# Routing the experts of a mixture layer through 25 passes of one ranking instead of 26 passes of two

## What is computed

```
gate = p_group * softmax(top_v)                  # top-2 inside the chosen group
hb   = silu(xb @ w_gate[e]) * (xb @ w_up[e])     # 1024 -> 512, rows xb of expert e
out[token] += gate * (hb @ w_down[e])            # 512 -> 1024
```

## Time and profile before

| | us |
|---|---|
| median of 3 runs | 1451.56 (1447.0 to 1452.16) |
| the profiled execution | 1454.74 |
| its span, first to last instruction | 1452.9 |
| PE busy in the span | 1336.4 (92%) |
| DVE, ACT, POOL busy | 506.4, 251.5, 175.2 |
| mean granted TensorE clock | 0.956 |

### The profile page before, as it was taken

The page is one execution under the profiler, slowest core; times in us unless marked ns, Lnnn a source line. Parts: engine busy times, 40 slices in busy tenths (PEclk is TensorE's granted clock), DMA queues, the critical chain, the costliest instruction groups (busy, mean ns, idle before and its releaser), DMA issues.

```text
span 1452.9 us, 15254 instructions
## 1 busy us (share of the span) xinstructions
PE 1336.4 (92%) x5616; PEld 691.3 (48%) x5616; DVE 506.4 (35%) x1193; ACT 251.5 (17%) x487; POOL 175.2 (12%) x170
## 2 busy tenths in 40 slices
PE   6999999999999888879998679999999999999985
PEld 3444554644446566654555534443444444444432
DVE  2079683133546565651344512111111111111100
ACT  5000114132124333331111010000000000000000
POOL 1000005222000000000000011211212112112111
PEclk9999999899999899999999589999999999999998
DMA  6011010100120110302221098959999999999970
GB/s 256 0 60 58 1 58 0 58 6 6 48 66 5 36 35 5 121 1 93 101 87 73 28 395 338 400 195 350 424 404 406 412 407 391 402 397 389 403 272 18
DMA packets 51272, 261.70 MB, mean 180 GB/s; under 512 B 21571, under 2 KB 21843, under 8 KB 38908
## 3 DMA queue, kind: packets, MB, share of 16 engines
q1 hardware_dynamic: 42684, 243.72, 41.9%
q0 software_dynamic: 8320, 16.81, 4.7%
q10 hardware_dynamic: 192, 0.17, 0.1%
HBM read 247.52 MB, written 23.64 MB: 187 GB/s over the span
## 4 chain that ended last, share of the span: by engine, by line
PE 69%; issue 8%; DMA 7%; DVE 7%; POOL 3%; DVEq 3%; ACT 1%; SPq 0%; POOLq 0%; ACTq 0%
PE ps L1176 18%; PE ps L1178 13%; PE ps L895 9%; PE ps L1081 8%; PE ps L899 4%; DMA arena<-in_ex_up 3%; PE ps L1026 3%; DMA arena<-in_ex_down 2%; PE ps L1057 2%; POOL arena L2020 2%; PE ps L1042 2%; PE ps L1162 1%; PE ps L1102 1%; DMA arena<-in_ex_gate 1%; DVE arena L1495 1%
## 5 line engine op out<-in xcount | busy, mean ns | idle before, releaser
L1176 PE MATMUL ps<-arena 128*128 128x512 f32 x768 | 336.7, 595 | 1.9 <-ACT arena L1971 0.8
L1176 PEld LDWEIGHTS ps<-arena 128*128 128x128 f32 x768 | 144.3, 191 | 171.9 <-issue 169.3
L1178 PE MATMUL ps<-arena 128*64 128x512 f32 x480 | 213.5, 601 | 8.3 <-DMA arena<-in_ex_up 4.5
L1179 PE MATMUL ps<-arena 128*64 128x512 f32 x480 | 213.6, 601 | 0.0
L899 PE MATMUL ps<-arena 128*128 128x512 f32 x384 | 173.6, 605 | 0.0
L895 PE MATMUL ps<-arena 128*128 128x512 f32 x320 | 137.6, 592 | 0.0
L1740 DVE TENSOR_TENSOR arena<-arena,ps 128x512 f32<-128x512 f32 x26 | 17.9, 689 | 328.8 <-PE ps L1176 202.3
L1178 PEld LDWEIGHTS ps<-arena 128*64 128x64 f32 x480 | 64.7, 138 | 138.1 <-issue 136.2
L1081 PE MATMUL ps<-arena 128*128 128x512 f32 x256 | 112.1, 597 | 0.8 <-DVE arena L1532 0.8
L899 PEld LDWEIGHTS ps<-arena 128*128 128x128 f32 x384 | 72.6, 195 | 83.0 <-issue 81.5
L2076 POOL DMA_INDIRECT out<-arena x26 | 42.0, 1615 | 473.2 <-DVE arena L1746 473.2
(11 more groups left out here) (299 smaller groups left out, 1297.7 us busy)
## 6 DMA issues: line engine op xcount, KB each, us to landing
arena<-in_ex_gate SPq DMA_DIRECT2D x32, 2048.0 KB, 21.7
arena<-in_ex_up SPq DMA_DIRECT2D x32, 2048.0 KB, 24.2
arena<-in_ex_down SPq DMA_DIRECT2D x32, 2048.0 KB, 24.0
arena<-in_w_in SPq DMA_DIRECT2D x5, 2048.0 KB, 7.8
arena<-in_x SPq DMA_DIRECT2D x16, 512.0 KB, 6.2
arena<-bias_by_distance SPq DMA_DIRECT2D x4, 1024.0 KB, 5.9
arena<-in_w_out SPq DMA_DIRECT2D x8, 512.0 KB, 7.3
out<-arena SPq DMA_DIRECT2D x8, 512.0 KB, 2.6
```

The lines of the kernel that those rows point to most:

```text
L1176: last = mm(ps[:, to, :], rowsT[:, k, :], weights[left][:, k, cols], **f)
L1178: mm(ps[0:HALF, to, :], rowsT[:, k, 0:HALF], weights[left][:, k, cols], **f)
L1179: last = mm(ps[HALF:P, to, :], rowsT[:, k, HALF:P], weights[right][:, k, cols], **f)
```

## The change

`PASSES` is now built by `expert_passes()` from one ranking over all 32 experts, in units of 64 rows. There are 25 passes: 14 "whole" (W) for ranks 0 to 13, and 11 two-sided ones. Four of these (R) hold rows 129 to 192 of ranks 0 to 3 in the left half and ranks 14 to 17 in the right; seven (P) hold ranks 18 to 31 and, in one place, 17 with 18, two by two. The order is W R W R W R P W R W P W W P W P W W W W P W P W P; the last pass is two-sided (ranks 30 and 31).

With one ranking a token's two experts can stand in the two halves of one pass, and so its output row could be added to twice by one DMA. Therefore a two-sided pass is added in two steps: `add_pass(n, 0)` adds the left rows, and `add_pass(n, 1)` the right ones after the first has landed. DVE makes the two lists of rows (`side_rows`, in which the rows of the other side are out of bounds and so are skipped). There are 36 adds where there were 26. Between the two steps POOL fetches the gates of the next pass. The next gather stands behind the second step.

```diff
+    for kind in "WRWRWRPWRWPWWPWPWWWWPWPWP":
+        if kind == "W":
+            rank = next(whole)
+            passes.append(("whole", (rank, 0), None))
+            if rank < 4:
+                rests.append((rank, 1))
+        elif kind == "R":
+            passes.append(("halves", rests.pop(0), (next(one), 0)))
+        else:
+            passes.append(("halves", (next(one), 0), (next(one), 0)))
...
+        def sides_of(n):
+            return (0,) if PASSES[n][0] == "whole" else (0, 1)
+
+        def landed_from(u, last):
+            return 16 * sum(len(sides_of(n)) for n in range(last + 1) if n % 2 == u)
...
-                pe.wait_ge(codeT_done, 3)
-                for n in range(2):
-                    last = mm(ps[:, 5, 40 * n:40 * n + RANKED], codeT[0:2 * EXPERTS, n, :], perm[0:2 * EXPERTS, :],
-                              start=True, stop=True)
-                last.then_inc(order_mm, 1)
+                pe.wait_ge(codeT_done, 2)
+                both = slice(0, 2 * EXPERTS)
+                mm(ps[:, 5, 0:NP], codeT[both, :], perm[both, EXPERTS:EXPERTS + NP], start=True, stop=True)
+                right = EXPERTS + NP
+                mm(ps[HALF:P, 5, N_WHOLE:NP], codeT[both, 0:HALF], perm[both, right:RANKED], start=True, stop=True).then_inc(order_mm, 1)
...
-            ts(slots[:, 0:16], ps[:, 5, 0:16], -1.0, None, ALU.add)
-            for side in range(2):
-                rows = slice(side * HALF, (side + 1) * HALF)
-                pairs = ps[rows, 5, 40:40 + RANKED].rearrange("p (s two) -> p s two", two=2)[:, 8:18, side]
-                ts(slots[rows, 16:NP], pairs, -1.0, None, ALU.add)
+            ts(slots[:, 0:NP], ps[:, 5, 0:NP], -1.0, None, ALU.add)
             nc.vector.drain()
             rows_of_blocks(0, NP)
             nc.vector.drain().then_inc(slots_ready, 1)
+            ts(not_left, cst[:, C_TOK:C_TOK + 1], float(HALF), 4.0 * SEQ, ALU.is_ge, ALU.mult)
+            nc.vector.drain()
+            ts(side_f[:, 0], tok_f[:, N_WHOLE:NP], not_left, None, ALU.add)
+            ts(side_f[:, 1], tok_f[:, N_WHOLE:NP], not_left, 4.0 * SEQ, ALU.subtract, ALU.add)
+            nc.vector.drain()
+            nc.vector.tensor_copy(side_rows, side_f)
+            nc.vector.drain().then_inc(sides_ready, 1)
...
-            f(codeT[0:2 * EXPERTS, 0, :], ps[0:2 * EXPERTS, 5, 128:256], ACT.Copy).then_inc(codeT_done, 1)
-            f(codeT[0:2 * EXPERTS, 1, :].rearrange("p (r n) -> p r n", r=2),
-              ps[0:2 * EXPERTS, 5, 128:128 + HALF].unsqueeze(1).to_broadcast([2 * EXPERTS, 2, HALF]), ACT.Copy).then_inc(codeT_done, 1)
+            f(codeT[0:2 * EXPERTS, :], ps[0:2 * EXPERTS, 5, 128:256], ACT.Copy).then_inc(codeT_done, 1)
...
-            def add_pass(n):
-                add_rows(n, n % 2, 16 * ((n + 1) // 2), rows_of(n))
+            def add_pass(n, side):
+
+                u = n % 2
+                rows = rows_of(n)
+                if len(sides_of(n)) == 2:
+                    pool.wait_ge(sides_ready, 1)
+                    rows = side_rows[:, side, COLUMN[n] - N_WHOLE:COLUMN[n] - N_WHOLE + 1]
+                pool.wait_ge(y_v, n + 1)
+                if side:
+                    pool.wait_ge(y_out[u], landed_from(u, n) - 16)
+                else:
+                    at_least(pool, y_out[1 - u], landed_from(1 - u, n - 1))
+                nc.gpsimd.indirect_dma_start(out, bass.IndirectOffsetOnAxis(ap=rows, axis=0), ys[:, u, :], None,
+                                             bounds_check=SEQ - 1, oob_is_err=False, compute_op=ALU.add).then_inc(y_out[u], 16)
...
                 if n:
-                    add_pass(n - 1)
+                    add_pass(n - 1, 0)
                     pool.wait_ge(row_gate_in, 16 * n)
                 fetch_gates(row_gate[:, n:n + 1], dst_of[:, COLUMN[n]:COLUMN[n] + 1])
+                if n and len(sides_of(n - 1)) == 2:
+                    add_pass(n - 1, 1)
+
             def last_pass():
-                add_pass(NP - 1)
-                pool.wait_ge(y_out[(NP - 1) % 2], 16 * ((NP - 1) // 2 + 1))
+                for side in range(len(sides_of(NP - 1))):
+                    add_pass(NP - 1, side)
+                pool.wait_ge(y_out[(NP - 1) % 2], landed_from((NP - 1) % 2, NP - 1))
```

More of the change, by code:

```diff
@@ L60, with expert_passes @@
 NCONST = C_EJ + 256
[L62 to L67, removed]
+def expert_passes():
+    whole, one, rests = iter(range(14)), iter(range(14, EXPERTS)), []
+    passes = []
+    for kind in "WRWRWRPWRWPWWPWPWWWWPWPWP":
[8 more added lines that the diff above has]
+            passes.append(("halves", (next(one), 0), (next(one), 0)))
+    return passes
+PASSES = expert_passes()
 NP = len(PASSES)
@@ L70, with experts_of @@
 SLOTS = NP + EXTRA
[L71 to L80, removed]
-def weight_loads():
[L85 to L89, removed]
+HALF = P // 2
+BLOCKS = {"whole": ((0, P, 0),), "halves": ((0, HALF, 0), (HALF, P, 1))}
+OF_KIND = {kind: [n for n in range(NP) if PASSES[n][0] == kind] for kind in BLOCKS}
+BY_KIND = OF_KIND["whole"] + OF_KIND["halves"]
+COLUMN = [BY_KIND.index(n) for n in range(NP)]
+N_WHOLE = len(OF_KIND["whole"])
+RANKED = EXPERTS + 2 * NP - N_WHOLE
+def experts_of(n):
+    return [side[0] for side in PASSES[n][1:] if side]
+def weight_loads():
+    order = list(dict.fromkeys(s for n in range(NP) for s in experts_of(n)))
+    last = [max(n for n in range(NP) if s in experts_of(n)) for s in order]
     issues = []
@@ L140, in order_constants @@
     part, e = np.arange(P)[:, None], np.arange(EXPERTS)[None, :]
[L141 to L147, removed]
+    mine, block = part % EXPERTS, part // EXPERTS
+    sides = ([(s, 0) for s in range(EXPERTS)] + [PASSES[n][1] for n in BY_KIND] + [PASSES[n][2] for n in BY_KIND[N_WHOLE:]])
+    rank = np.array([s for s, _ in sides])[None, :]
+    of_block = np.array([b for _, b in sides])[None, :]
+    cols = [np.broadcast_to(EXPERTS - 1.0 - e, (P, EXPERTS)), (e == mine), np.where(block == of_block, rank, -1)]
     return np.ascontiguousarray(np.concatenate([np.asarray(c, np.float32) for c in cols], 1))
@@ L797, in _ @@
             sp.wait_ge(extras_ready, 1)
+            sp.wait_ge(down_mm, NP)
             def extra_weights(slot, u, pair):
@@ L1199, in down @@
                 at_least(pe, y_v, n)
-                left, right = landed_for("down", n)
+                blocks = landed_for("down", n)
                 for half in range(2):
-                    last = times_weights(5 + half, actT, FC, w_down, left, right, slice(half * 512, (half + 1) * 512))
+                    last = times_weights(5 + half, actT, FC, w_down, blocks, slice(half * 512, (half + 1) * 512))
                 last.then_inc(down_mm, 1)
@@ L1229, in extra @@
                 for half in range(2):
-                    last = times_weights(5 + half, actT, FC, w_down, u, u, slice(half * 512, (half + 1) * 512))
+                    last = times_weights(5 + half, actT, FC, w_down, [(0, P, u)], slice(half * 512, (half + 1) * 512))
                 last.then_inc(down_mm, 1)
```

101 lines of the change are left out of this document (55 added, 46 removed).

## The result

| | before | change |
|---|---|---|
| median, us | 1451.86 (4 runs, 1447.0 to 1455.32) | **1426.68** (4 runs, 1426.49 to 1429.05) |
| the profiled execution | 1454.74 | 1429.05 |
| its span | 1452.9 | 1427.2 |

Two later sets of runs of the same kernel gave 0.985 twice (1428.77 and 1428.13 us); by those two medians the time would lie just inside the range, at its lower end.

The account below looks back on a forecast made before the run. PE was taken as the bound by a small margin over the weight stream. Terms -22.2 + 2 - 0.6 + 0 + 6 = -14.8 us, from the median 1451.56 us, gave 1437 us, range 1428 to 1448 us.

Parts of the forecast that it names:

- the waits that were expected in the last pass: Last, two-sided pass: PE waits 0 to 5 us for up of rank 31 and 1 to 3 us for its down.
- the end (+6): After PE's last product: two one-sided adds instead of one, +3.5 us, plus pass 23's add; +6 us, bounds +3.5 and +11.
- the add of pass 23: Ahead of the last add: issued some 10 us before the last y_v, landing in 12.5 us, it costs 2.5 us.
- One pass fewer on PE, -22.2: Expert stretch on PE: 25 passes instead of 26, all else equal, save 22.2 us.
- Another order of the weights, +2: Weight stream: buffers come free at other times, waits total about 14 us instead of 11.8; +2 us, bounds -3 and +6.
- the four waits: PE waits for up and down of rank 18 in pass 6, and for up and down of rank 31 in the last.
- Start, -0.6: Before the first gather: one ACT copy and two DVE operations leave the path; -0.6 us, bounds -1 and +0.5.
- Ten more adds, 0: POOL's chain of 36 adds, 13.3 us each, stays hidden beside PE; 0 us, bounds 0 and +5.
- The sum of -20: Alternative total by the skill page's DMA formula: one-sided add 2.3 us, end +1 instead of +6, sum -20 instead of -15.
- Nothing is given back: Rival: PE's pass is won, no waits in the last pass, pass 23's add early; -22.3, 1429 us, chance 0.12.
- The stream did not take over: Rival on the weight stream: pieces come at 5.95 us instead of 5.8, PE waits in the last pass; 1447 us, chance 0.16.
- the chain of adds: Rival on POOL: 36 steps of 16.3 us make adds the bound, PE waits for rows; 1469 us, chance 0.06.

Follow-up runs that it names:

- before again: The kernel before, run once more unchanged for a second profile: 1454.02 us in a single run.
- before with eight fetches more: The kernel before with eight more indirect transfers on GpSimd, fetching the gates of passes 10 to 17 a second time: 1451.23 us, ratio 1.000.
- before less one pass: The kernel before without its second pass for rows 129 to 192 of ranks 2 and 3, so 25 passes: 1431.22 us, ratio 0.987.

## Why the prediction was wrong

The direction and the main mechanism were right. Two steps failed, both the same way: the waits that were expected in the last pass (in the term of +2), and the end (+6), in which the add of pass 23 was priced at 2.5 us and the drain was missing.

**One pass fewer on PE, -22.2.** Right as a mechanism (22.22 us a pass measured), a little small: taking a pass out of the old order gives 23.5 to 24.5, since some waiting and slow clock go with it. Against that kernel the change's PE part is 1 to 2 us longer. Counted so, the pass was priced too low and the order about right; counted as below, from 22.2 us a pass, the order was priced too high. The sum of the two terms is off by 2.2 us either way.

**Another order of the weights, +2.** PE's part as a whole was forecast at -22.2 + 2 = -20.2; the two profiles of before and the three of the change give 599.6 and 577.2 us in the mean, -22.4. The step that failed is the waits of the last pass, "up of rank 31 (0 to 5 us) and its down (1 to 3 us)": none came, and the waits for weights are 6.0 us in all where 9 to 12 were expected. The stream was as forecast, up of rank 31 landed at 1384.0 us (1024 + 62 x 5.8 = 1383.6). PE was what the replay had too early: it asked for that matrix at 1387.5 us, and for the last down, landed at 1400.1, at 1402.9. Its two waits in pass 6 were forecast well (1.2 us for 1 to 2, 4.8 for 3.3, 1.5 of clock for 1.8), and together they hold PE up for 7.5 us. Without those 7.5 us PE would have asked at 1380.0 and waited 4 us for up of rank 31, within the forecast's 0 to 5. So the four waits seem to have been added up as if they were independent; this is worked out from the times and no run tests it.

**Start, -0.6.** From the last copy on ACT's path to the first gather it is 4.57 us instead of 5.11, -0.5, as forecast. The gather then landed in 5.5 us instead of 4.6 and took that back. The other 3.4 us by which the change's profile starts earlier arise around 430 to 510 us, in the mixers, which no edit touches. The terms that the marks show add up to -22.4 + 2.0 - 0.5 = -20.9. The medians of the change lie 25.2, 23.2 and 22.8 us under those of before in its three sets; the intervals of the ratios take in the 20.9, but all three medians lie beyond it. The starts, 3 us apart in the mean between old tables and new, would fill the distance; whether that is chance stays open.

**Ten more adds, 0.** Right: PE never waits for a gather beyond that of the start, the median landing is 12.3 us, and the late second steps cost nothing. The one place where adds may cost something is one that the forecast had not named, the stretch before pass 6's down matrix, whose landing is 1 to 3 us later with them. That would be inside the bound of +5.

**The end, +6.** The landings were as priced: from PE's end to the last landing 12.5 us instead of 8.1, +4.4, with 4.55 and 4.46 us for the one-sided adds where 4.6 each was taken. The add of pass 23 was issued at 1403.6 us and landed 6.1 us later, not 12.5, at 1409.7, ahead of PE's end; the 2.5 us for it were not paid. The failed step is what the sum ended with: "from the last product to the last landing" is not the end of the program. Behind it lies GpSimd's drain, and that is 2.3 us shorter in the change. Net +1.7 to +2.1.

Of the Trainium skill's estimate, page "DMA: Bandwidth & Descriptors", section "Anatomy of one DMA" (2.3 us for a one-sided add), the trace leaves nothing: the two take 4.55 and 4.46 us in a nearly quiet queue. Nor is 2.3 us quite what the page's formula gives: an estimated 2.1 us for 15 rows of 4 KB, 2.6 for 64. The sum of -20 by it came nearer to the result than -15, but by luck: what made up the distance were the missing waits, the add of pass 23 and the drain.

**The rivals.** "Nothing is given back", 1429 us at 0.12, is what the time looks like. The missing waits at the end and the early add of pass 23 came true; the drain it did not know, so that part of its nearness is luck. The stream did not take over (64 pieces landed between 1033.1 and 1400.1 us, 5.73 us each), and the chain of adds bound only when every pass had two steps.

## What to carry to other kernels

Follow the chain to the last instruction of the program, not to the last landing: the drain of the engine that issued the indirect DMAs was 4 to 7 us here and changed with the program. In a replay with two near bounds, a wait that is forecast early moves every later demand back, so the waits are not independent terms; let each one shift the clock of the replay before the next is priced. Extra transfers cost nothing here where the stream was ahead, and seem to delay it by 1 to 3 us where it was the bound; a wait there can cost its length and a fall of TensorE's clock on top. Compare several profiles of the same kernel before a difference of 4 us in one is explained: two kernels that had done the same work up to then stood 3.5 us apart.

## What the runs showed of the hardware

**GpSimd's last drain grows with the number of indirect DMAs issued**, 0.08 us each: 6.32 us with 75 (two kernels, one with 64-row adds and one with 128-row adds last), 6.57 with 78 (two kernels), 6.97 with 83, 7.22 with 86. The size of the last adds does not matter. In all the kernels with every two-sided pass in two steps it is 3.0 us shorter than this line, with the same slope: 4.19 to 4.24 us with 86, 5.38 with 100. What takes the 3.0 us away is open: not the number of transfers (86 stands on both sides), nor whether the last add is whole or one-sided (4.19 with a whole one). Those kernels have 36 or 50 adds, the others 25 to 33.

**A fall of the clock is not one price, and does not follow from the length of the wait alone.** In pass 6 the 1.2 GHz level came behind each wait of 4.0 to 4.8 us and not behind the one of 2.9 us; the product behind it took 8.42 to 10.08 us in nine profiles and 7.09 without the fall, so a fall cost 1.3 to 3.0 us. In the old order, at the wait for down near 945 us, the clock fell behind 2.8 us, and behind 2.4 and 2.5 in before again and in before with eight fetches more; in before less one pass it did not fall behind 2.4 us at the same place. What decides is open.
